# Two-block hybrid forward pass on one core: clamps, squares and probability scaling move to ScalarE, branch counts become logarithms in the mask, and the SSD head buffers rotate through four places

## The chip, the cores and the metric

The kernel runs on one core of a Trainium2 chip. The metric is the device time of one execution in microseconds (us), lower is better. One core has TensorE (PE in the profile, with PEld for its weight loads), VectorE (DVE), ScalarE (ACT), GpSimd (POOL) and the queue of SyncE (SP) that issues the weight DMAs. All engines run their own instruction streams and meet only at semaphores.

## What is computed

An input of 256 tokens by 1024 features goes through two blocks. The parts of the reference that the change touches, in short:

```python
# first block, Mamba-2 SSD: 32 heads in 4 groups, chunks of 128 tokens
cs = cumsum(dA)                                     # per head, along the tokens
lmat = exp(where(i >= j, cs_i - cs_j, -inf))        # decays between tokens i and j
y = einsum(cb, lmat, xdt) + ...                     # 256 x 256 per head, lower triangle
# first block, RG-LRU: width 1280 = 10 blocks of 128
a_t = exp(log_a)
b_t = sqrt(-expm1(2 * log_a)) * (i_gate * u)        # needs a_t squared
h_t = a_t * h_{t-1} + b_t
# second block, two layers, each with retention, a top-k attention (DSA, 4 heads)
# and a dilated attention (8 heads, three patterns (128,1), (512,4), (2048,16))
for window, dilation in DIL_PATTERNS:
    p = exp(s - m); den = sum(p); o = p @ v / den; lse = m + log(den)
alpha = softmax(lses); o = sum(alpha * outs)
# which is one softmax in which key j counts as often as patterns reach it:
# p_j = count_j * exp(s_j - m) / sum_j count_j * exp(s_j - m)
```

Both blocks also have large projections (in, out, FFN). They make up nearly all of the arithmetic.

## The kernel before

**Weight tiles.** Every projection is cut into 191 tiles of at most 128 x 2048 fp32 values (`TILES`), in one order for the whole program. A tile arrives by DMA in one of three `raw` slots. ScalarE copies it to `w_hi` (a rounded fp32r value), then VectorE and GpSimd each compute a part of the rest, `w_lo = raw - w_hi`; `POOL_SHARE` says in eighths how much of a tile GpSimd takes. TensorE then makes each product three times (hi*hi, hi*lo, lo*hi): 48 matmuls of 128x256 for a full tile. `w_hi` and `w_lo` have three slots, and `LEAD` is 2: the split of tile i+2 waits for tile i-1 to be used up (`tile_used`).

**Order.** ScalarE, VectorE and GpSimd each go through `walk`: for tile i first `lead(i)` (the split of tile i+2), then `rest` (second half of the evacuation of tile i-1), then the stages that `stage_order` puts at "mid" of tile i, then `evac` (first half of the evacuation of tile i), then the "after" stages. TensorE does the stages of "mid" between the halves of its tile. Each engine works strictly in its program's order, so a wait holds everything behind it.

**The LRU stages** (tiles lx 1 to bc 3). For each of 10 blocks ScalarE computes two tanh, `lru_a` (exp) and another tanh; GpSimd squares `lru_a` into a half of `tmp[4]`; VectorE makes `lru_b` and a gated `lru_u` of them.

**The SSD stages** (tiles gate 0 to z 4). For each group g of 8 heads there are `ssd_load` (a DMA on ScalarE's queue that broadcasts the group's cumulative sums to all partitions in `cs_all`), `ssd_open` and four pairs of heads, one pair per tile: `ssd_decay(g, p)` builds the two heads' decays in two buffers of `tmp`, and one tile later TensorE's `ssd_val(g, p)` (8 small matmuls from `tmp` and `xdt`) uses them and VectorE's `ssd_val` adds the result into `xbc`. In `ssd_decay` VectorE computes min(cs_j - cs_i, 0) (two `ts` per head), ScalarE takes exp in place, and VectorE multiplies by the masked scores `cb_mask`. The buffer index is `2 + (2 * q + h) % 4` with q = 4g + p and h = 2p or 2p + 1, which comes to `tmp[2]` for every even head and `tmp[3]` for every odd one.

**The attention stages** (from tile dil_v 0 of each layer to out_2 1). There are three sets of four heads: "dil0", "dsa" and "dil1". `att(l, a, step)` runs over steps 0 to 5, each at another tile:
- steps 0 and 2: TensorE computes the scores of two heads, VectorE scales them, adds the mask (`c["union"]` or `keep`) and takes the negative row maximum, ScalarE takes exp.
- steps 1 and 3: VectorE normalises. For the dilated sets it first multiplies by the table `count` (0 to 3) with a row sum, then takes a reciprocal and multiplies the probabilities by it; for dsa the row sum comes with ScalarE's exp.
- steps 2 and 4: TensorE transposes the probabilities, ScalarE copies them to `probs_t`; steps 3 and 5: product with the values and evacuation.

At "mid" of tile dil_k 1 of a layer stand retention steps and `att(l, "dil0", 1)`; at "mid" of dil_q 1, `att(l, "dil0", 2)` and `att(l, "dsa", 0)`. VectorE's evacuation of tile dil_k 1 (`lk_t<-bank,rstd` in the profile) comes between the two. Semaphores are shared between kinds (`GOES_ON`), which only renames a wait.

In the profile all ScalarE activations have line L856, VectorE's tensor-tensor operations L1182, tensor-scalar L1186 and L1187, scalar-tensor-tensor L1190, GpSimd's L1705, matmuls L491 and transposes L499.

## Time and profile before

| | |
|---|---|
| median of 3 runs | 1372.14 us (1369.8 to 1372.83) |
| the profiled execution | 1372.57 us, of which the span of the trace is 1371.3 us |
| TensorE busy | 1256.6 us (92%) |
| VectorE busy | 922.8 us (67%) |
| ScalarE busy | 614.1 us (45%) |
| GpSimd busy | 475.3 us (35%) |
| mean granted TensorE clock | 0.957 of full |

How to read it: the span is 1.3 us shorter than the execution's own time, and what follows is worked out on the span. TensorE's busy share is high, but it is an average. The first block's small stages (from 40 to 320 us) and the attention stages (720 to 810 us and 1080 to 1172 us) have gaps in it; in the FFN stretches there are nearly none.

### The profile page before, as it was taken

How to read it: one execution, taken by the hardware profiler on the slowest of the kernel's cores; microseconds unless marked ns; L12 is line 12 of the kernel's file. 1: busy time of each engine (PE TensorE's matmuls, PEld its weight loads, DVE VectorE, ACT ScalarE, POOL GpSimd, SP SyncE). 2: the span in 40 equal slices, each digit the busy share in tenths (PEclk: the TensorE clock that was granted, in tenths of full speed). 3: DMA queues.
4: the chain of work that ended last, by engine and by line, in shares of the span. 5: the costliest groups of instructions: out<-in, count | busy, mean ns of one | idle time of the engine just before them, and what ended most of it. 6: DMA issues, size and time to landing. Idle time of an engine off the chain costs nothing.

```text
span 1371.3 us, 23257 instructions
## 1 busy us (share of the span) xinstructions
PE 1256.6 (92%) x9852; PEld 1213.1 (88%) x9852; DVE 922.8 (67%) x1246; ACT 614.1 (45%) x703; POOL 475.3 (35%) x170
## 2 busy tenths in 40 slices
PE   4998898898998999999987899999999878999996
PEld 3988788888998999999886789999999767999996
DVE  5789987886646655557688856555456796755554
ACT  5766443445634533335433454333344245533332
POOL 1644233446773211111544233222224442422221
PEclk9999899999999999999998999999989989999998
DMA  8434444443466555555334136555543323455540
GB/s 249 156 97 152 153 155 154 154 149 112 170 210 209 180 182 181 181 182 151 124 112 134 62 103 206 184 184 185 163 154 123 124 86 98 145 195 181 183 160 31
DMA packets 153974, 209.57 MB, mean 153 GB/s; under 512 B 7536, under 2 KB 134672, under 8 KB 153232
## 3 DMA queue, kind: packets, MB, share of 16 engines
q1 hardware_dynamic: 150080, 201.54, 45.3%
q10 hardware_dynamic: 3792, 6.55, 1.4%
q8 instruction: 78, 1.28, 0.4%
q14 instruction: 24, 0.20, 0.0%
HBM read 207.00 MB, written 1.08 MB: 152 GB/s over the span
## 4 chain that ended last, share of the span: by engine, by line
PE 64%; DVE 20%; ACT 8%; issue 5%; POOL 1%; DMA 0%; ACTq 0%; SPq 0%; DVEq 0%; POOLq 0%
PE bank L491 63%; ACT w_hi L856 3%; DVE w_lo L1182 3%; DVE xbc L1190 2%; DVE probs_dil L1190 2%; ACT tmp L856 2%; DVE tmp L1187 1%; PE bank L499 1%; DVE lru_u L1190 1%; DVE tmp L1190 1%; DVE tmp L1182 1%; POOL w_lo L1705 1%; ACT act_hi L856 1%; DVE residual L1182 1%; DVE work L1186 1%
## 5 line engine op out<-in xcount | busy, mean ns | idle before, releaser
L491 PE MATMUL bank<-act_hi,w_hi 128*128 128x256 f32 x2920 | 849.9, 291 | 34.3 <-DVE w_lo L1182 14.6
L491 PE MATMUL bank<-act_lo,w_hi 128*128 128x256 f32 x2920 | 836.7, 287 | 0.0
L491 PE MATMUL bank<-act_hi,w_lo 128*128 128x256 f32 x2920 | 835.6, 286 | 0.0
L491 PEld LDWEIGHTS bank<-act_hi,w_hi 128*128 128x128 f32 x2920 | 571.8, 196 | 47.2 <-issue 36.6
L491 PEld LDWEIGHTS bank<-act_lo,w_hi 128*128 128x128 f32 x2920 | 571.9, 196 | 1.1 <-issue 0.5
L491 PEld LDWEIGHTS bank<-act_hi,w_lo 128*128 128x128 f32 x2920 | 571.1, 196 | 0.0
L1182 DVE TENSOR_TENSOR w_lo<-raw,w_hi 128x2048 fp32r<-128x2048 f32 (+4 forms) x179 | 375.6, 2100 | 264.8 <-ACT w_hi L856 264.7
L856 ACT ACTIVATE w_hi<-raw 128x2048 fp32r<-128x2048 f32 (+1 forms) x191 | 360.5, 1890 | 373.2 <-PE bank L491 371.8
L1705 POOL TENSOR_TENSOR w_lo<-raw,w_hi 128x1280 fp32r<-128x1280 f32 (+6 forms) x94 | 318.7, 3394 | 433.9 <-ACT w_hi L856 433.9
L1705 POOL TENSOR_TENSOR act_lo<-tmp,act_hi 128x512 fp32r<-128x512 f32 x52 | 133.3, 2570 | 407.0 <-ACT act_hi L856 407.0
L1182 DVE TENSOR_TENSOR tmp<-bank,rstd 128x512 f32<-128x512 f32 x43 | 29.7, 691 | 52.6 <-PE bank L491 52.5
L856 ACT ACTIVATE tmp<-tmp 128x384 f32<-128x384 f32 (+1 forms) x48 | 25.6, 555 | 70.5 <-DVE tmp L1187 69.7
L856 ACT ACTIVATE act_hi<-tmp 128x512 fp32r<-128x512 f32 x55 | 34.1, 619 | 34.0 <-DVE tmp L1190 34.0
L491 PE MATMUL bank<-w_hi,act_hi 128*128 128x256 f32 (+1 forms) x128 | 37.8, 295 | 3.1 <-DVE lq_t L1182 3.1
L856 ACT ACT_TABLE_LOAD x28 | 35.9, 1283 | 4.0 <-issue 2.3
L491 PE MATMUL bank<-w_hi,act_lo 128*128 128x256 f32 (+1 forms) x128 | 36.4, 285 | 0.0
L491 PE MATMUL bank<-w_lo,act_hi 128*128 128x256 f32 (+1 forms) x128 | 36.4, 284 | 0.0
L1190 DVE SCALAR_TENSOR_TENSOR probs_dil<-probs_dil,consts 128x128 f32<-128x128 f32 (+1 forms) x32 | 36.2, 1168 | 0.0
L1190 DVE SCALAR_TENSOR_TENSOR xbc<-bank,params,xbc 128x255 f32<-128x255 f32 (+2 forms) x72 | 29.0, 473 | 3.7 <-ACT xbc L856 3.7
L1190 DVE SCALAR_TENSOR_TENSOR tmp<-tmp 128x512 f32<-128x512 f32 x43 | 30.4, 708 | 1.1
L491 PEld LDWEIGHTS bank<-w_hi,act_hi 128*128 128x128 f32 x128 | 26.0, 203 | 5.8 <-DVE lq_t L1182 3.9
L491 PE MATMUL bank<-tmp,xdt 128*64 128x256 f32 (+1 forms) x128 | 15.3, 360 | 17.0 <-DVE tmp L1182 12.1
(206 smaller groups left out, 903.3 us busy)
## 6 DMA issues: line engine op xcount, KB each, us to landing
raw<-in_w_in SPq DMA_DIRECT2D x64, 1024.0 KB, 5.3
raw<-in_w_up SPq DMA_DIRECT2D x32, 1024.0 KB, 5.4
raw<-in_w_down SPq DMA_DIRECT2D x32, 1024.0 KB, 4.9
raw<-in_w_ffn_in SPq DMA_DIRECT2D x22, 1024.0 KB, 5.1
raw<-in_w_out SPq DMA_DIRECT2D x12, 1024.0 KB, 4.9
raw<-in_w_ffn_out SPq DMA_DIRECT2D x11, 1024.0 KB, 4.9
raw<-in_w_out_ssm SPq DMA_DIRECT2D x8, 1024.0 KB, 4.8
raw<-in_w_out_lru SPq DMA_DIRECT2D x5, 1024.0 KB, 4.8
```

Source lines behind the costliest of these rows:

```text
L491: return mm_ops.matmul(out, lhs, rhs, start=start, stop=stop, skip_group_check=True)
L499: return mm_ops.transpose(out, a, c["ident"][0:k, 0:k])
L856: return ops.activation(out, a, func, bias=bias, scale=scale, accum_out=accum)
L1182: return ops.tensor_tensor(out, a, b, op)
L1186: return ops.tensor_scalar(out, a, s1, None, op0)
L1187: return ops.tensor_scalar(out, a, s1, s2, op0, op1)
L1190: return ops.scalar_tensor_tensor(out=out, in0=a, scalar=s, in1=b, op0=op0, op1=op1, accum_out=accum)
L1705: return nc.gpsimd.tensor_tensor(out, a, b, op)
```

## The change

It does five things.

1. **Decays on ScalarE.** In `ssd_decay` ScalarE computes Relu(cs_i - cs_j) itself (two activations per head, scale -1, the column of `cs_tok` as bias) and then exp with scale -1. VectorE keeps only the product with `cb_mask`. `neg_cs` becomes `cs_tok`.
2. **Four places.** The buffers of a pair are `tmp[2 + h % 4]`: pairs alternate between `tmp[2], tmp[3]` and `tmp[4], tmp[5]`. ScalarE waits for the value product of the pair before the last one only.
3. **Squares on ScalarE.** The square of `lru_a` is an activation right behind the last tanh; GpSimd has no `lru` stage left.
4. **Counts as logarithms.** The mask `union` holds log(count), so exp gives count * exp(s - m) at once, with its row sum from ScalarE's accumulator. The table `count` and VectorE's product with it go away.
5. **Scaling on ScalarE.** VectorE takes only the reciprocal of the sums (`_r`); ScalarE multiplies the probabilities by it (`_n`), for all three sets of heads.

```diff
@@ build, buffers of a pair (PE, ACT and DVE alike) @@
-                    e = tmp[2 + (2 * q + h) % 4]
+                    e = tmp[2 + h % 4]
@@ act_program: lru @@
                 fn(r, r, ACT.Tanh, scale=lam, bias=lam).then_inc(*tick("lru_tl"))
+                act.wait_ge(*at("lru_b", h - 1))
+                fn(tmp[4][:, (h % 2) * SEQ:(h % 2 + 1) * SEQ], lru_a[:, h, :], ACT.Square).then_inc(*tick("lru_sq"))
@@ act_program: ssd_decay @@
                 q = 4 * g + p
+                act.wait_ge(sem("cs_broadcast"), 16 * (g + 1))
+                act.wait_ge(*at("dt_tok", 1))
+                act.wait_ge(*at("ssd_val", q - 1))
                 for h in (2 * p, 2 * p + 1):
-                    e = tmp[2 + (2 * q + h) % 4]
+                    e, hh = tmp[2 + h % 4], g * HPG + h
+                    fn(e[:, 0:SEQ], cs_all[:, h, :], ACT.Relu, scale=-1.0, bias=cs_tok[:, 0, hh:hh + 1])
+                    fn(e[:, SEQ:KQ], cs_all[:, h, P:SEQ], ACT.Relu, scale=-1.0, bias=cs_tok[:, 1, hh:hh + 1]).then_inc(
+                        *tick("ssd_d"))
+                for h in (2 * p, 2 * p + 1):
+                    e = tmp[2 + h % 4]
                     act.wait_ge(*at("ssd_d", HPG * g + h + 1))
-                    fn(e[:, 0:KQ], e[:, 0:KQ], ACT.Exp).then_inc(*tick("ssd_e"))
+                    fn(e[:, 0:KQ], e[:, 0:KQ], ACT.Exp, scale=-1.0).then_inc(*tick("ssd_e"))
@@ act_program: att @@
                         for n, x, y in PAIRS:
-                            inst = fn(p[:, x:y], p[:, x:y], ACT.Exp, bias=st[:, n:n + 1],
-                                      accum=None if dilated else st[:, 2 + n:3 + n])
+                            inst = fn(p[:, x:y], p[:, x:y], ACT.Exp, bias=st[:, n:n + 1], accum=st[:, 2 + n:3 + n])
                         inst.then_inc(*tick(f"{a}_e"))
+                if step in (1, 3):
+                    for h in heads[step - 1:step + 1]:
+                        s = 4 * l + h - heads[0]
+                        p, st = probs[a][s % 4], stats[a][s % 4]
+                        act.wait_ge(*at(f"{a}_r", s + 1))
+                        for n, x, y in PAIRS:
+                            inst = fn(p[:, x:y], p[:, x:y], ACT.Copy, scale=st[:, 4 + n:5 + n])
+                        inst.then_inc(*tick(f"{a}_n"))
@@ vec_program: ssd_decay @@
                 for h in (2 * p, 2 * p + 1):
-                    e, hh = tmp[2 + (2 * q + h) % 4], g * HPG + h
-                    vec.wait_ge(sem("cs_broadcast"), 16 * (g + 1))
-                    vec.wait_ge(*at("ssd_val", q - 1))
-                    ts(e[:, 0:SEQ], cs_all[:, h, :], neg_cs[:, 0, hh:hh + 1], ALU.add, 0.0, ALU.min)
-                    ts(e[:, SEQ:KQ], cs_all[:, h, P:SEQ], neg_cs[:, 1, hh:hh + 1], ALU.add, 0.0, ALU.min).then_inc(
-                        *tick("ssd_d"))
-                for h in (2 * p, 2 * p + 1):
-                    e = tmp[2 + (2 * q + h) % 4]
+                    e = tmp[2 + h % 4]
@@ vec_program: att @@
                         vec.wait_ge(*at(f"{a}_e", s + 1))
-                        if dilated:
-                            for n, x, y in PAIRS:
-                                inst = stt(p[:, x:y], p[:, x:y], 1.0, c["count"][:, x:y], ALU.mult, ALU.mult,
-                                           accum=st[:, 2 + n:3 + n])
-                            inst.then_inc(*tick("dve_step"))
-                            vec.wait_ge(*now("dve_step"))
-                        ops.reciprocal(st[:, 4:6], st[:, 2:4]).then_inc(*tick("dve_step"))
-                        vec.wait_ge(*now("dve_step"))
-                        for n, x, y in PAIRS:
-                            inst = ts(p[:, x:y], p[:, x:y], st[:, 4 + n:5 + n], ALU.mult)
-                        inst.then_inc(*tick(f"{a}_n"))
+                        ops.reciprocal(st[:, 4:6], st[:, 2:4]).then_inc(*tick(f"{a}_r"))
@@ pool_program @@
-            def lru(h):
-                pool.wait_ge(*at("lru_a", h + 1))
-                pool.wait_ge(*at("lru_b", h - 1))
-                tt(tmp[4][:, (h % 2) * SEQ:(h % 2 + 1) * SEQ], lru_a[:, h, :], lru_a[:, h, :], ALU.mult).then_inc(*tick("lru_sq"))
@@ shape_constants @@
-        "union": pairs(np.where(cnt > 0, 0.0, MASKED)), "count": pairs(cnt),
+        "union": pairs(np.where(cnt > 0, np.log(np.maximum(cnt, 1)), MASKED)),
```

How the instructions stand now. The first place is ScalarE's stream in the SSD stages, at tile ly 0, as a piece of the difference; `cs_all` and `cs_tok` are the cumulative sums, `tmp_2` to `tmp_5` the decays of a pair, `w_hi` the split of the tile two ahead.

```order
 L856 ACTIVATE w_hi_2<-raw_2 128x2048 [waits raw_arrived_2]
 L856 ACTIVATE tmp_0<-tmp_0 128x512 [waits ly_arg]
-L856 ACTIVATE tmp_2<-tmp_2 128x384 [waits ssd_d]
-L856 ACTIVATE tmp_3<-tmp_3 128x384 [waits ssd_d]
+L856 ACTIVATE tmp_4<-cs_all,cs_tok 128x256 [waits ssd_val]
+L856 ACTIVATE tmp_4<-cs_all,cs_tok 128x128
+L856 ACTIVATE tmp_5<-cs_all,cs_tok 128x256
+L856 ACTIVATE tmp_5<-cs_all,cs_tok 128x128
```

The two exps waited for VectorE (`ssd_d`); now four activations stand in front of them, of which the first waits for TensorE (`ssd_val`), and the exps follow in the new buffers.

The second place is VectorE's stream at "mid" of tile dil_k 1 and "mid" of dil_q 1 in the attention of the first layer, before:

```order
L1182 TENSOR_TENSOR ro_t<-ro_t,bank_3 128x256 [waits ro,gn_mean]
L1190 SCALAR_TENSOR_TENSOR probs_dil0_0,small<-probs_dil0_0,consts_2 128x128 [waits ssd_e]
L1190 SCALAR_TENSOR_TENSOR probs_dil0_0,small<-probs_dil0_0,consts_2 128x256
L1639 RECIPROCAL small<-small 128x2 [waits dve_step]
L1186 TENSOR_SCALAR probs_dil0_0<-probs_dil0_0,small 128x128 [waits dve_step]
L1186 TENSOR_SCALAR probs_dil0_0<-probs_dil0_0,small 128x256
...
L1182 TENSOR_TENSOR lk_t<-bank_1,rstd 128x512 [waits tile_used]
L1603 RECIPROCAL rq_t<-rq_t 128x256 [waits ly_tanh]
L1190 SCALAR_TENSOR_TENSOR rq_t<-rq_t,params,rg_t 128x256 [waits rg,dve_step]
```

And the same place after the change (the line numbers are those of the changed file):

```order
L1199 TENSOR_TENSOR ro_t<-ro_t,bank_3 128x256 [waits ro,gn_mean]
L1643 RECIPROCAL small<-small 128x2 [waits ssd_e] x2
L1199 TENSOR_TENSOR lk_t<-bank_1,rstd 128x512 [waits tile_used]
L1613 RECIPROCAL rq_t<-rq_t 128x256 [waits ly_tanh]
L1207 SCALAR_TENSOR_TENSOR rq_t<-rq_t,params,rg_t 128x256 [waits rg,dve_step]
```

Ten instructions of two heads are two now, and the evacuation `lk_t` stands right behind them.

The third place is ScalarE's stream at "mid" of tile dil_v 1, in the second layer, as a piece of the difference.

```order
 L856 ACTIVATE act_hi<-bank_6 128x256 [waits dil0_o]
-L856 ACTIVATE probs_dil1_0<-probs_dil1_0,small 128x128 [waits z_arg]
-L856 ACTIVATE probs_dil1_0<-probs_dil1_0,small 128x256
-L856 ACTIVATE probs_dil1_1<-probs_dil1_1,small 128x128 [waits z_arg]
-L856 ACTIVATE probs_dil1_1<-probs_dil1_1,small 128x256
+L856 ACTIVATE probs_dsa_0<-probs_dsa_0,small 128x128 [waits lru_gu]
+L856 ACTIVATE probs_dsa_0<-probs_dsa_0,small 128x256
+L856 ACTIVATE probs_dsa_1<-probs_dsa_1,small 128x128 [waits lru_gu]
+L856 ACTIVATE probs_dsa_1<-probs_dsa_1,small 128x256
```

Four scalings of dsa stand ahead of the exps of dil1, which now also write their row sums.

## Rows read from the trace of the kernel before

**Rows 1.** The page of the profile, TensorE's busy time and the chain that ended last.

```profile
PE 1256.6 (92%) x9852; PEld 1213.1 (88%) x9852; DVE 922.8 (67%) x1246; ACT 614.1 (45%) x703; POOL 475.3 (35%) x170
...
PE 64%; DVE 20%; ACT 8%; issue 5%; POOL 1%; DMA 0%; ACTq 0%; SPq 0%; DVEq 0%; POOLq 0%
```

**Rows 2.** Waits of the whole program: total us, times, longest.

```profile
ACT tmp L856 <- DVE tmp L1187: 69.7, 16, 5.0
...
PE bank L491 <- DVE lk_t L1182: 14.3, 2, 7.2
...
PE bank L499 <- ACT probs_t L856: 6.9, 2, 3.5
```

**Rows 3.** Four stretches: length, busy time of each engine, granted clock (PEclk), DMA.

```profile
157.00:306.00 149.00, 132.46 (x1024) 124.49 (x1024) 125.38 (x182) 66.01 (x89) 57.42 (x18) 0.94 0.47 149
315.70:322.50 6.80, 3.12 (x10) 2.76 (x11) 4.96 (x6) 6.59 (x9) 4.59 (x3) 0.50 0.51 157
745.80:756.00 10.20, 6.27 (x26) 4.00 (x27) 8.92 (x23) 3.63 (x8) 1.59 (x2) 0.50 0.38 130
203.00:207.00 4.00, 4.00 (x36) 4.00 (x35) 3.72 (x2) 0.18 (x1) 2.40 (x1) 1.00 0.04 14
```

**Rows 4.** Timeline of ScalarE, VectorE and GpSimd, one SSD step (199 to 208.5 us).

```profile
199.66 0.99 ACT L856 ACTIVATE tmp<-tmp 128x384 f32<-128x384 f32 x2 [3.26 <-DVE tmp L1187]
...
201.27 1.91 ACT L856 ACTIVATE w_hi<-raw 128x2048 fp32r<-128x2048 f32 x1
...
203.25 2.40 POOL L1705 TENSOR_TENSOR w_lo<-raw,w_hi 128x1024 fp32r<-128x1024 f32 x1 [5.77 <-ACT w_hi L856]
...
203.28 3.46 DVE L1182 TENSOR_TENSOR w_lo<-raw,w_hi 128x1024 fp32r<-128x1024 f32 x1 [2.03 <-ACT w_hi L856]
...
206.66 0.47 DVE L1190 SCALAR_TENSOR_TENSOR xbc<-xbc,params,bank 128x256 f32<-128x256 f32 x1
...
207.05 1.00 DVE L1187 TENSOR_SCALAR tmp<-cs_all,neg_cs 128x256 f32<-128x256 f32 x4
...
207.62 0.98 ACT L856 ACTIVATE tmp<-tmp 128x384 f32<-128x384 f32 x2 [4.44 <-DVE tmp L1187]
```

**Rows 5.** TensorE's waits, 160 to 307 us and 315 to 325 us.

```profile
PE bank L491 <- DVE tmp L1182: 12.5, 12, 2.0
...
PE bank L491 <- DVE tmp L1182: 6.1, 1, 6.1
```

**Rows 6.** Timeline of VectorE, GpSimd and TensorE in the first layer's attention.

```profile
737.60 4.70 DVE L1190 SCALAR_TENSOR_TENSOR probs_dil<-probs_dil,consts 128x128 f32<-128x128 f32 x1
...
742.23 4.71 DVE L1190 SCALAR_TENSOR_TENSOR probs_dil<-probs_dil,consts 128x256 f32<-128x256 f32 x1
...
747.65 0.28 DVE L1190 SCALAR_TENSOR_TENSOR probs_dil<-probs_dil,consts 128x128 f32<-128x128 f32 x1
...
748.99 0.68 DVE L1182 TENSOR_TENSOR lk_t<-bank,rstd 128x512 f32<-128x512 f32 x1
...
737.52 9.14 POOL L1705 TENSOR_TENSOR w_lo<-raw,w_hi 128x2048 fp32r<-128x2048 f32 x2 [8.03 <-ACT w_hi L856]
...
749.73 1.22 PE L491 MATMUL bank<-rk_t,consts 128*128 128x256 f32 x2 [7.17 <-DVE lk_t L1182]
```

**Rows 7.** Timeline of ScalarE in the same attention, and at tile lx 4.

```profile
739.13 0.41 ACT L856 ACTIVATE rk_t<-ro_t 128x256 f32<-128x256 f32 x1
...
754.44 1.49 ACT L856 ACTIVATE probs_dil<-probs_dil,small 128x128 f32<-128x128 f32 x4
...
772.01 0.80 ACT L856 ACTIVATE probs_dil<-probs_dil,small 128x128 f32<-128x128 f32 x2 [5.02 <-DVE small L1626]
...
61.20 0.47 ACT L856 ACTIVATE tmp<-bank,params 128x256 f32<-128x256 f32 x1 [0.66 <-PE bank L491]
```

**Rows 8.** Groups by line: busy us, mean ns, idle before them.

```profile
L1190 DVE SCALAR_TENSOR_TENSOR probs_dil<-probs_dil,consts 128x128 f32<-128x128 f32 (+1 forms) x32 | 36.2, 1168 | 0.0
...
L1187 DVE TENSOR_SCALAR tmp<-cs_all,neg_cs 128x256 f32<-128x256 f32 x64 | 22.9, 418 | 0.0
...
L1705 POOL TENSOR_TENSOR tmp<-lru_ab 128x256 f32<-128x256 f32 x10 | 10.5, 1053 | 13.2 <-ACT lru_ab L856 13.2
...
L856 ACT ACTIVATION_READ_ACCUMULATOR probs_dsa<-probs_dsa,small 128x1 f32 x16 | 3.1, 196 | 0.0
```

More of the change, by code:

```diff
@@ L82 @@
 CONSTS_2 = [("rotate", P), ("cos", SEQ), ("sin", SEQ), ("cos_k", SEQ), ("sin_k", SEQ), ("decay", RET_H * SEQ),
-            ("causal", KQ), ("union", KQ), ("count", KQ)]
+            ("causal", KQ), ("union", KQ)]
 def tile_names():
@@ L277 @@
     "dil0_pt": ("xbc_tanh", 12), "dsa_e": ("gate", 8), "dsa_hi": ("mix_hi", 4),
-    "ckv_n": ("cs", 1), "dil0_p": ("ssd_d", 32), "dil0_max": ("ssd_m", 32), "dil0_n": ("ssd_y", 16),
-    "dil0_lo": ("lru_out", 5), "dsa_p": ("lru_scan", 10), "dsa_max": ("lru_b", 10), "dsa_n": ("lru_gu", 10),
-    "dsa_lo": ("gn_x", 8), "dil1_p": ("z", 8), "dil1_max": ("z_arg", 8), "dil1_n": ("ly_arg", 5),
+    "ckv_n": ("cs", 1), "dil0_p": ("ssd_xdt", 8), "dil0_max": ("ssd_m", 32), "dil0_n": ("n1_sq", 4), "dil0_r": ("ssd_y", 16),
+    "dil0_lo": ("lru_out", 5), "dsa_p": ("lru_scan", 10), "dsa_max": ("lru_b", 10), "dsa_n": ("x1_hi", 4), "dsa_r": ("lru_gu", 10),
+    "dsa_lo": ("gn_x", 8), "dil1_p": ("z", 8), "dil1_max": ("z_arg", 8), "dil1_n": ("sp_exp", 2), "dil1_r": ("ly_arg", 5),
     "dil1_lo": ("ly_gelu", 5), "sel_acc": ("xbc", 12),
@@ L366, in build @@
         dt_tok = sb("dt_tok", [P, TT, HEADS], stack=one)
-        neg_cs = sb("neg_cs", [P, TT, HEADS], stack=one)
+        cs_tok = sb("cs_tok", [P, TT, HEADS], stack=one)
         lru_w = xbc[:, 0:2 * LC * P // SEQ, :].rearrange("p k (a j) -> p (k a) j", j=P).rearrange(
@@ L1354, in dt_turn @@
                 ops.tensor_copy(dt_tok[:, :, :], view[:, 0])
-                ts(neg_cs[:, :, :], view[:, 1], -1.0, ALU.mult).then_inc(*tick("dt_tok"))
+                ops.tensor_copy(cs_tok[:, :, :], view[:, 1]).then_inc(*tick("dt_tok"))
             def lru(h):
@@ L1630, in att @@
                         s = 4 * l + h - heads[0]
[L1631 removed]
+                        st = stats[a][s % 4]
                         vec.wait_ge(*at(f"{a}_e", s + 1))
[L1633 to L1643 removed]
+                        ops.reciprocal(st[:, 4:6], st[:, 2:4]).then_inc(*tick(f"{a}_r"))
                 if step in (3, 5):
@@ L1758, in pool_program @@
             low_part(4, 2, pair(tmp[8][:, :])).then_inc(*tick("x1_lo_pool"))
-            walk(lead, lambda i, name, j: None, rest, {"lru": lru, "norm_split": norm_split, "lru_split": lru_split,
-                                                       "ret": ret, "final": final})
+            walk(lead, lambda i, name, j: None, rest, {"norm_split": norm_split, "lru_split": lru_split, "ret": ret,
+                                                       "final": final})
         pe_program()
```

1 line of the change is left out of this document (removed).

## The prediction, made before the changed kernel ran

> **What bounds the kernel now.** The page comes first: TensorE is busy for 92% of the span and has 64% of the chain that ended last, but VectorE has 20% of that chain and ScalarE 8% [rows 1]. So most of the time is matmul time, which the change does not touch (TensorE's program is the same), and what can be won are the places where TensorE stands still or runs at the lower clock. The waits say where these are. ScalarE waited 69.7 us in 16 pieces for the clamps of the SSD decays (one for each pair of heads), TensorE 14.3 us in two pieces for `lk_t` and 6.9 us in two for `probs_t`, once in each layer [rows 2].
>
> The SSD stretch from 157 to 306 us is 149.0 us long, and TensorE is busy for 132.5 of them, so it idles 16.5 us. The granted clock is 0.94 there, which is 1.2 instead of 2.4 GHz for 12% of the time, 17.9 us; TensorE is busy for 89% of that and loses half, 8.0 us [rows 3]. Together 24.5 us could be had at most. TensorE's waits for the masked decays are 12.5 us of it, and one more of 6.1 us stands behind the stretch [rows 5].
>
> Why it idles is read from one step [rows 4]. ScalarE's `w_hi` starts at 201.27 and takes 1.91. VectorE's and GpSimd's `w_lo` start together at 203.25, and VectorE's takes 3.46 where GpSimd's takes 2.40: VectorE waits for GpSimd and then does its own part. Then come the product's addition to `xbc` (0.47), the clamps, and at 207.62 the exps, before which ScalarE had waited 4.44. The next `w_hi` stands behind these exps. The exps are 7.96 us apart (199.66 to 207.62): it is a ring through ScalarE, GpSimd and VectorE, and not TensorE, that sets the pace. TensorE's own work for such a step is 48 large matmuls, at 36 in 4.00 us [rows 3] 5.3 to 5.8 us, and the 8 small ones, for which I put 1.0: 6.8 us. The ring is 1.2 us longer.
>
> In the attention the picture is one of blocking. GpSimd splits two tiles back to back for 9.14 us from 737.52. VectorE's products with `count`, which read two tensors of SBUF, take 4.70 and 4.71 us in that time, and 0.28 when GpSimd is idle. So `lk_t` comes only at 748.99 and TensorE, which needs its bank, stands still for 7.17 us [rows 6]. Behind it the clock is 0.50 for 10.2 us [rows 3].
>
> **The change part by part.**
>
> *What goes from VectorE.* 64 clamps, 22.9 us, and 32 products with `count`, 36.2 us [rows 8]; with the 48 scalings, at 0.28 each as the nearest of their size [rows 6] 13.4, it is 72 us of 923. *What comes to ScalarE.* No activation with this input existed; the nearest are four exps of 128 and 256 columns in SBUF with a per-partition operand, 1.49 us [rows 7]. 16 pairs of decays are 23.8 us, 48 scalings 17.9 us, 10 squares at 0.41 are 4.1 us, and 32 reads of the accumulator at 0.196 [rows 7, 8] are 6.3 us: 52 us on 614. Bounds: if the clamp costs nothing beyond its cover, 0; if each costs what a lone 128x256 one does, 0.41, it is 64 x 0.41 = 26 us.
>
> *SSD: the ring breaks.* ScalarE's clamps wait only for TensorE's product two pairs back, because there are four buffers. So exps no longer wait for VectorE, and the next `w_hi` starts when TensorE has used up a tile. ScalarE's work for a step is then 1.91 + 1.49 + 0.98 and an evacuation, for which I put 0.9, 5.3 us, and 6.0 with another tanh, below TensorE's 6.8. VectorE has, after `w_hi`, 3.46 + 0.47 + 1.0 for the masked product, 4.9 us. Both fit, and TensorE becomes the bound. I take 14.0 of the 16.5 us of idle time and 6.0 of the 8.0 us of clock: 20.0. The two buffers alone would change little, the waits are for VectorE and not for a buffer. The wait of 6.1 us behind it [rows 5] hangs on ScalarE reaching the square root of the first group's norm, which stands behind the last exps; these exps waited for clamps that GpSimd blocked. I put it down to 1.4, so 4.7 more. **SSD: -24.7 us.** From both sides: 12 if only the clamps' own time (16 x 1.0, less what was hidden) goes from the ring, 30 if every gap closes and the clock's 1.6 us at 315.7 [rows 3] go too.
>
> *Attention, each layer.* Two reciprocals of two columns stand where 11.4 us of products and scalings stood (737.60 to 748.99 [rows 6]), so `lk_t` follows TensorE at once and 7.2 us go. The half clock behind it costs half of 6.27 busy us, 3.1. ScalarE's four scalings (1.49) delay the `w_hi` behind them, which has room: GpSimd works until 746.7 on the two splits. The wait for `probs_t` (3.5) is that of ScalarE for the maxima of dil1, 5.02 us [rows 7], that is for a VectorE that was late; it is less late, but ScalarE has eight more scalings (3.0 us) in front of these exps, which I see eat part. I take 2.5 of 3.5. Later ScalarE's scalings of dsa and dil1 stand four to a half tile of TensorE, and I count 1.0 us back for them. 7.2 + 3.1 + 2.5 - 1.0 = 11.8, **two layers: -23.6 us.** Bounds: 7.2 a layer, if the clock and the second wait stay and 1.0 more is lost (12), and 14 a layer (28).
>
> What could be late next: VectorE's `rq_t` product with `rg_t`, also of two SBUF tensors, now reaches the place of GpSimd's splits earlier. If it starts behind the start of a split, it waits up to 4.7 us as the `count` products did. That is the risk to the second wait.
>
> *LRU.* GpSimd loses 10 squares (10.5 us) and ScalarE gains 4.1 us. In tiles lx 3 and lx 4 ScalarE has two blocks in a tile and only 0.66 us of waiting in front [rows 7], so 2 x 0.41 comes through once or twice, and its `w_hi` and the softplus behind it get later. VectorE is blocked less by GpSimd. **+1.5 us**, from -1 to +3.
>
> *Everything else* (FFN, projections) has the same instructions; the mask with logarithms costs the same addition as the one of zeros.
>
> The sum is -24.7 - 23.6 + 1.5 = -46.8 us. I take off 2.8 for waits that take the place of those that go and that I can't name: -44. Against the profiled execution's 1372.6 that is 1328.6; the median of the three runs is 0.4 lower, so **1328 us**.
>
> Two rules of the Trainium skill bear on it. "GPSIMD Engine Reference", section "8. Key points", says that GpSimd shares its SBUF interfaces with VectorE and contends with instructions that have two SBUF inputs or run in the two-port mode; the 4.70 against 0.28 us above is such a case, and the clamps are of the second kind. "ScalarE: Activation LUTs", section "Rules for kernel authors", speaks against the change: relu and multiplication belong on VectorE. By rows, four clamps took 1.00 there [rows 4] and I give ScalarE 1.49; going by this rule the sum would be 16 x 0.49 = +7.8 us for the clamps, which would hold if both engines were equally full.
>
> **The rivals.**
>
> *A. Only one of the two parts pays (20%).* The attention's gain is eaten by ScalarE's order: `w_hi` and `probs_t` stand behind scalings that wait for a reciprocal, which waits for a blocked VectorE instruction. For it: 4.7 us for each such block. Against: in the trace the blocked products stand behind the sums, which are there early. Then 1372.6 - 24.7 + 1.5 = 1349, and about the same if instead the SSD keeps its pace.
>
> *B. The split sets the pace (9%).* GpSimd's and VectorE's `w_lo` stay serial at 3.46, and TensorE's waits turn to `w_lo`. Then the ring loses only the clamps, 12 us, and in the attention, where GpSimd splits whole tiles, VectorE's next two-tensor instruction takes the blocked one's place: 1372.6 - 12 + 1.5 = 1362. Against: `w_lo` is made two tiles ahead.
>
> *C. ScalarE becomes the bound (6%), slower.* All its 52 us of added work lie on the path, in the SSD tiles with a tanh and in the attention: 1328.6 + 52 = 1380. It decides for slower from 44 us exposed, and in the SSD from a step of ScalarE above 7.96 us; it is 5.3 to 6.0 by rows. (The rule on VectorE for relu in "ScalarE: Activation LUTs" of the Trainium skill points this way.)
>
> *D. No change (3%).* VectorE's relief all lies beside matmuls. The 7.17 us wait speaks against it.
>
> **How the numbers follow.** The forecast has 62%, with its own range of 1318 to 1342 from the bounds of its parts. For 8 in 10 the range reaches down to 1316 (every gap and clock piece gone, and LRU's -1) and up to 1352, over case A. A measurement of this kernel can tell about 0.2%, 2.7 us. Faster by more: 62 + 20 + 9, less 1 for B ending there, 90%; within it 4%; slower 6%.
>
> **What would show it.** In the new trace: ScalarE's waits for VectorE's clamps gone and its exps 6.8 us apart; TensorE's 7.17 us waits for `lk_t` under 1 us and full clock behind them; VectorE near 850 us, ScalarE near 665; waits for `probs_t` 1 us each. The prediction would be wrong if TensorE waits for `w_hi` or `w_lo` in the SSD, if a blocked VectorE instruction stands before each reciprocal, or if four clamps or scalings cost above 2.5 us.

## The result, and the profile after

The changed kernel takes 1314.25 us (median of 4 runs, 1314.09 to 1314.49), the kernel before 1371.66 on the same chip (4 runs, 1369.8 to 1372.83). The ratio is 0.958, 95% interval 0.957 to 0.960: 57.4 us faster, where 44 were forecast, and 1.8 us below the range's lower end of 1316. One execution of `ssd_only` below took 5210 us where its other four took 1339 to 1342, a slow state of the chip, and is left out of its numbers.

The page of the changed kernel, the lines that answer to [rows 1], with the granted clock in 40 slices between them:

```profile
PE 1235.0 (94%) x9852; PEld 1196.2 (91%) x9852; DVE 847.4 (65%) x1070; ACT 657.1 (50%) x857; POOL 464.3 (35%) x160
...
PEclk9999899999999999999889999999989899999998
...
PE 78%; DVE 13%; ACT 6%; issue 2%; DMA 1%; POOL 0%; ACTq 0%; SPq 0%; DVEq 0%; POOLq 0%
```

TensorE runs the same 9852 matmuls, but is busy for 21.6 us less than before: that is time at 1.2 GHz that became time at 2.4 (the clock's records have 118 us at the lower level before and 63 after). Its idle time is the span less the busy time: 1371.3 - 1256.6 = 114.7 before, 1313.2 - 1235.0 = 78.2 after, 36.5 less. So the 58.1 us of the span are 36.5 of idle time and 21.6 of clock. VectorE is busy for 75 us less, part of it time in which it was held up, and ScalarE for 43 more.

TensorE's waits in the changed kernel (total us, times, longest):

```profile
PE bank L491 <- DVE w_lo L1199: 17.0, 7, 4.3
PE bank L491 <- DVE tmp L1199: 13.7, 4, 9.0
PE bank L491 <- ACT act_hi L856: 10.4, 2, 7.6
PE bank L491 <- DVE rq_t L1199: 7.6, 2, 3.8
PE bank L491 <- DVE act_lo L1207: 5.3, 8, 1.1
PE bank L499 <- DVE act_lo L1199: 4.0, 4, 1.8
```

Against [rows 2] the waits for `lk_t` (14.3) and for `probs_t` (6.9) are gone, those for `tmp` fell from 31.3 to 13.7 in the whole program, 12.5 + 6.1 of the 31.3 in the SSD [rows 5], and ScalarE's 69.7 us for the clamps stand in no row any more. The waits for `act_lo` at transposes (L499) rose from 1.1 to 4.0, 1.8 of them at one place in each layer that had 0.6 before, and those for `w_lo` from 14.6 to 17.0, none of them in the SSD.

The SSD in windows (columns as in [rows 3]); the first stretch is nearly seven tiles long:

```profile
190.80:237.40 46.60, 46.60 (x389) 43.95 (x388) 38.13 (x35) 33.39 (x61) 21.97 (x8) 1.00 0.57 178
160.00:291.00 131.00, 130.07 (x1076) 123.10 (x1077) 113.56 (x126) 90.86 (x153) 61.88 (x21) 1.00 0.57 180
```

TensorE's value products, one group in each step, stand 6.75 us apart:

```profile
201.96 0.88 PE L491 MATMUL bank<-tmp,xdt 128*64 128x256 f32 x8
...
208.71 0.88 PE L491 MATMUL bank<-tmp,xdt 128*64 128x256 f32 x8
```

So it is for eleven of the twelve steps within the groups of heads (the last one has 7.61); before, they were 7.4 to 9.5 us apart. ScalarE's exps are 4.7 to 8.2 us apart, since it now runs ahead. In the first window TensorE is busy all the time at the full clock, ScalarE for 72% (4.8 us of a step) and VectorE for 82% (5.5). And one step's timeline, to be laid beside [rows 4]:

```profile
213.42 1.91 ACT L856 ACTIVATE w_hi<-raw 128x2048 fp32r<-128x2048 f32 x1
...
215.41 3.46 POOL L1705 TENSOR_TENSOR w_lo<-raw,w_hi 128x1536 fp32r<-128x1536 f32 x1 [3.24 <-ACT w_hi L856]
...
215.43 3.98 DVE L1199 TENSOR_TENSOR w_lo<-raw,w_hi 128x512 fp32r<-128x512 f32 x1 [1.39 <-ACT w_hi L856]
...
219.33 0.47 DVE L1207 SCALAR_TENSOR_TENSOR xbc<-xbc,params,bank 128x256 f32<-128x256 f32 x1
...
220.97 0.84 ACT L856 ACTIVATE lru_ab<-bank,params 128x256 f32<-128x256 f32 x2 [5.64 <-PE bank L491]
...
223.50 1.49 ACT L856 ACTIVATE tmp<-cs_all,cs_tok 128x256 f32<-128x256 f32 x4
...
224.88 0.93 ACT L856 ACTIVATE tmp<-tmp 128x384 f32<-128x384 f32 x2
```

The split still stands in a row: VectorE's quarter of `w_lo` takes 3.98 us beside GpSimd's 3.46. It no longer matters, because ScalarE does not come back to VectorE for its clamps: its idle time now ends with TensorE (5.64), and the exps follow the clamps at once.

TensorE's 9852 matmuls stand in the same order in both traces, so each stretch can be cut at the start of the same matmul in both. What became shorter (a minus is longer), in us:

| stretch of the kernel before | shorter by | of it idle time | of it busy time (clock) | forecast: idle, clock |
|---|---|---|---|---|
| 0 to 152.0 (with the LRU) | -2.7 | -3.7 | 1.0 | -1.5 |
| 152.0 to 326.6 (SSD) | 30.8 | 21.3 | 9.5 | 18.7, 6.0 |
| 326.6 to 704.3 | -1.5 | 0.0 | -1.5 | none |
| 704.3 to 803.9 (attention) | 14.6 | 9.25 | 5.3 | 8.7, 3.1 |
| 803.9 to 1062.0 | 1.6 | 0.0 | 1.5 | none |
| 1062.0 to 1166.1 (attention) | 15.1 | 9.25 | 5.8 | 8.7, 3.1 |

The two windows of the second row are these, the kernel before first:

```profile
152.00:326.61 174.61, 151.15 (x1148) 142.02 (x1149) 143.89 (x201) 81.97 (x105) 68.71 (x23) 0.92 0.47 151
```

```profile
154.70:298.48 143.78, 141.64 (x1148) 134.17 (x1149) 125.66 (x137) 102.88 (x169) 68.53 (x23) 0.98 0.56 180
```

### The profile page after: what moved, and what is told of

Same layout as the page of the kernel before. It is cut to its first block, busy times and chain, and to the rows that moved or that the text cites. A ratio compares the mean times of both kernels' runs of the same rounds, so it can differ in the third digit from the quotient of the medians.

```text
span 1313.2 us, 23221 instructions
## 1 busy us (share of the span) xinstructions
PE 1235.0 (94%) x9852; PEld 1196.2 (91%) x9852; DVE 847.4 (65%) x1070; ACT 657.1 (50%) x857; POOL 464.3 (35%) x160
## 4 chain that ended last, share of the span: by engine, by line
PE 78%; DVE 13%; ACT 6%; issue 2%; DMA 1%; POOL 0%; ACTq 0%; SPq 0%; DVEq 0%; POOLq 0%
PE bank L491 77%; DVE w_lo L1199 2%; ACT w_hi L856 2%; DVE xbc L1207 1%; ACT tmp L856 1%; ACT act_hi L856 1%; ACT L856 1%; PE bank L499 1%; DVE residual L1199 1%; DVE work L1203 1%; DVE act_lo L1207 1%; DVE tmp L1199 1%; DVE score L1199 1%; DVE rk_t L1199 1%; DVE tmp L1207 1%
## 5 line engine op out<-in xcount | busy, mean ns | idle before, releaser
L491 PE MATMUL bank<-act_hi,w_hi 128*128 128x256 f32 x2920 | 847.7, 290 | 36.5 <-DVE w_lo L1199 17.0
L1199 DVE TENSOR_TENSOR tmp<-tmp 128x512 f32<-128x512 f32 x28 | 20.4, 730 | 13.7 <-ACT tmp L856 12.1
L856 ACT ACTIVATE probs_dil<-probs_dil,small 128x128 f32<-128x128 f32 x64 | 26.2, 447 | 5.9 <-DVE small L1636 5.3
L856 ACT ACTIVATE tmp<-residual 128x512 f32<-128x512 f32 x32 | 18.5, 621 | 20.5 <-DVE residual L1199 13.6
```

What stands on the lines that cost most here:

```text
L491: return mm_ops.matmul(out, lhs, rhs, start=start, stop=stop, skip_group_check=True)
L856: return ops.activation(out, a, func, bias=bias, scale=scale, accum_out=accum)
L1199: return ops.tensor_tensor(out, a, b, op)
```

## The experiments

Fifteen further kernels ran, one of them the changed kernel again, on four chips and in 4 to 12 executions each. Each is compared with the kernel before on the same chip (its median was 1371.9 to 1373.0). A gain in us is the ratio's distance from 1, times 1372.

### Each part alone

`att_only` is the kernel before with the logarithms of the counts and ScalarE's scalings; `ssd_only` has ScalarE's decays and the four places; `squares_only` the LRU's squares on ScalarE; `no_squares` is the changed kernel with the squares back on GpSimd:

```diff
+            def lru(h):
+                pool.wait_ge(*at("lru_a", h + 1))
+                pool.wait_ge(*at("lru_b", h - 1))
+                tt(tmp[4][:, (h % 2) * SEQ:(h % 2 + 1) * SEQ], lru_a[:, h, :], lru_a[:, h, :], ALU.mult).then_inc(*tick("lru_sq"))
```

> The kernel before with the attention's part of the change alone (counts in the mask as logarithms, ScalarE scales the probabilities). Theory (the parts add, each gap of TensorE closes together with the low clock behind it): the trace of the changed kernel moves by 14.6 and 15.0 us in the two attentions, so 1371.7 - 29.6 = 1342. The prediction's own term was 23.6: 1348. Rival A (the parts need each other: ScalarE's scalings stand behind blocked VectorE instructions): 1372 to 1360.

> The kernel before with the SSD's part alone (decays on ScalarE, four places). Theory: everything from 157 us to the end of the SSD closes, all 16.5 us of idle time and the clock's pieces, 28 to 30 us: 1371.7 - 29 = 1343, with 1347 by the prediction's term of 24.7. Rival (the split sets the pace, as VectorE's and GpSimd's halves of w_lo stay serial): 12 us, 1360. Rival (ScalarE's clamps cost more than put down and stretch the LRU tiles' end): gain below 20, above 1352.

> The kernel before with the ten LRU squares on ScalarE alone. Theory: +1.5 us, 1373, of which the first gap behind the first LRU matrix product is 1.2 (in the changed kernel's trace it is 2.77 against 1.58), and the rest of the shift by clock. Rival (GpSimd's squares block VectorE, so their move gains): 1371.7 - 3 = 1369. Rival (no change): 1371.7.

> The changed kernel with the ten LRU squares back on GpSimd. Theory: the squares cost 1.5 to 2.7 us on ScalarE, so 1314.3 - 2 = 1312.3, faster than the changed kernel. Rival (relief of GpSimd is part of what the SSD gained, as the excess over the prediction is there): 1317 or more. Rival (no effect): 1314.3.

| kernel | median us | ratio to before | 95% interval |
|---|---|---|---|
| att_only | 1340.9 | 0.9771 | 0.9755 to 0.9787 |
| ssd_only | 1340.8 | 0.9769 | 0.9754 to 0.9784 |
| squares_only | 1372.6 | 0.9996 | 0.9983 to 1.0009 |
| no_squares | 1312.4 | 0.9565 | 0.9552 to 0.9579 |

Either part pays by itself, 31.4 and 31.7 us, as the two theories had it from the changed kernel's trace, so rival A (only one pays) falls, and with it B (the split sets the pace, 12 us for the SSD) and D (no change). The sum of the two, 63.1, is 3.4 more than both together give (59.7), which is no more than the three intervals leave open.

The squares alone make no difference that the times can tell, and taking them out of the changed kernel gives 0.9565 against 0.9583, with intervals that overlap. The traces can tell. From the matmul that starts at 60.0 us in the kernel before to the one at 152.0, all seven traces with the squares on ScalarE take 1.0 to 1.3 us longer than the kernel before, and the nine others without them differ from it by less than 0.2. TensorE's longest wait for `w_lo` there, in the kernel before, in `squares_only` and in the changed kernel:

```profile
95.28 0.55 PE L491 MATMUL bank<-act_hi,w_hi 128*128 128x256 f32 x1 [3.37 <-DVE w_lo L1182]
```

```profile
96.59 0.36 PE L491 MATMUL bank<-act_hi,w_hi 128*128 128x256 f32 x1 [3.97 <-DVE w_lo L1184]
```

```profile
98.02 0.55 PE L491 MATMUL bank<-act_hi,w_hi 128*128 128x256 f32 x1 [3.98 <-DVE w_lo L1199]
```

That is 0.6 us more behind a `w_hi` that stands behind one more activation of 0.4, and another 0.6 stands at the tile before, at 85 us. So the squares cost 1.2 us, by the way that the prediction named. The kernel without them, `no_squares`, is the better one.

Windows over the same matmuls show what went. First the kernel before, 1002 matmuls of the SSD with the wait behind it and the first attention with 602, then the same 1002 in `ssd_only`, and 603 in `att_only`:

```profile
177.65:326.61 148.96, 128.94 (x1002) 121.56 (x1001) 121.49 (x165) 69.77 (x89) 60.44 (x20) 0.94 0.45 146
...
704.30:803.90 99.60, 81.84 (x602) 71.99 (x601) 78.50 (x186) 42.08 (x73) 37.42 (x10) 0.90 0.33 106
```

```profile
173.11:295.82 122.71, 121.64 (x1002) 115.45 (x1001) 106.02 (x110) 86.13 (x140) 58.98 (x20) 1.00 0.55 176
```

```profile
704.20:789.20 85.00, 76.48 (x603) 68.38 (x601) 49.66 (x130) 51.65 (x113) 37.81 (x10) 0.96 0.38 124
```

In the SSD idle time (length less busy) falls from 20.0 to 1.1, by 18.9, and busy time by 7.3. In the attention idle time falls from 17.8 to 8.5, by 9.2, and busy time by 5.4. The forecast had 18.7 of idle time in the SSD (14.0 + 4.7) and 8.7 in a layer's attention (7.2 + 2.5 - 1.0): close, but the forecast's SSD began at 157 us and this window at 177.65; from 152 us on, the idle time of `ssd_only` falls by 20.7 and its busy time by 10.0 (21.3 and 9.5 in the changed kernel, as in the table above). The forecast had 6.0 and 3.1 of clock: too little.

### The attention's two halves

`counts_only` puts the logarithms into the mask, drops the products with `count` and leaves the scalings on VectorE. `scale_only` moves the scalings and keeps the products; the two edits together are `att_only`:

```diff
 # counts_only, VectorE
-                        if dilated:
-                            for n, x, y in PAIRS:
-                                inst = stt(p[:, x:y], p[:, x:y], 1.0, c["count"][:, x:y], ALU.mult, ALU.mult,
-                                           accum=st[:, 2 + n:3 + n])
```

> The kernel before with the counts moved into the mask as logarithms alone; VectorE still scales the probabilities. Theory (an instruction on two tensors of SBUF or in the two-port mode waits for GpSimd's split to end, and the scalings are such instructions): the scalings take the blocked place and most of the wait for lk_t stays, so a gain of 5 to 15 us of the 31.4 of both: 1373 - 10 = 1363. Rival (the products with count are the whole cost, the scalings run unblocked): 1373 - 29 = 1344.

> The kernel before with the scalings on ScalarE alone; VectorE still multiplies by count and sums. Theory: the two blocked products of 4.7 us stay, only what stood behind them goes, so TensorE's wait for lk_t falls from 7.2 us by at most 2 in each layer: 1373 - 4 = 1369. Rival (either half of the edit frees VectorE enough): 1373 - 20 = 1353.

1363.7 us (0.994, 0.993 to 0.995) and 1366.1 us (0.996, 0.994 to 0.997): 8.4 and 5.9 us, where both edits together gave 31.4. VectorE's timeline of `counts_only`, at the place of [rows 6]:

```profile
735.58 0.16 DVE L1633 RECIPROCAL small<-small 128x2 f32<-128x2 f32 x1
735.77 9.15 DVE L1186 TENSOR_SCALAR probs_dil<-probs_dil,small 128x128 f32<-128x128 f32 x2
...
745.50 0.68 DVE L1182 TENSOR_TENSOR lk_t<-bank,rstd 128x512 f32<-128x512 f32 x1
```

Two scalings take 9.15 us where the two products had taken 4.70 and 4.71; the next two, at 745.03 with GpSimd idle, take 0.55. So those 9.4 us did not belong to the product but to whatever instruction of that kind came first beside GpSimd's two splits, and TensorE's wait for `lk_t` falls from 7.17 to 5.51 us only. In `scale_only` another thing happens:

```profile
737.45 4.67 DVE L1198 SCALAR_TENSOR_TENSOR probs_dil<-probs_dil,consts 128x128 f32<-128x128 f32 x1
...
742.05 0.41 DVE L1198 SCALAR_TENSOR_TENSOR probs_dil<-probs_dil,consts 128x256 f32<-128x256 f32 x1
...
746.22 4.74 DVE L1198 SCALAR_TENSOR_TENSOR rk_t<-rq_t,ro_t 128x256 f32<-128x256 f32 x1
```

One product is held up and the second is not, because ScalarE's scalings stand in front of the `w_hi` of the next tile and wait for this blocked VectorE: GpSimd's second split starts at 746.13, not right behind the first. The wait for `lk_t` falls to 1.65 us, not by "at most 2" as expected, but the late split now holds up `rk_t`, and TensorE waits 4.16 us for `lq_t` where it had waited 0.78. This is the mechanism of rival A, and it takes back more than half of what `lk_t` gained. With both edits nothing is left beside the first split that could be held up: in `att_only` TensorE waits 0.78 us for `lq_t` and for `lk_t` not at all. That is why the gain of the two small edits together is more than twice their sum. The Trainium skill, "SBUF — State Buffer", section "SBUF: two separate sides", has it as an exclusive lock between GpSimd and a VectorE instruction that runs in a two-port mode or reads two SBUF inputs, which whichever of the two starts first holds for its whole instruction; the two times 4.6 us, each one split long, agree.

`dil_unsplit` takes the other way out. It is the kernel before, with GpSimd's splits taken away and the products left:

```diff
-              "dsa_q": 5, "ret_k": 5, "ret_q": 5, "ret_v": 5, "ret_g": 5, "dil_k": 7, "dil_q": 7, "dil_v": 8,
-              "out_2": 8}
+              "dsa_q": 5, "ret_k": 5, "ret_q": 5, "ret_v": 5, "ret_g": 5, "dil_k": 0, "dil_q": 0, "dil_v": 0,
+              "out_2": 0}
```

> The kernel before with the w_lo of dil_k, dil_q, dil_v and out_2 made by VectorE alone, so that GpSimd splits nothing beside the products with count; VectorE has 10 x 2.1 - 1.7 = 19 us more in each layer. Theory (blocking): the products take 0.28 and 0.42 us, TensorE's wait for lk_t falls from 7.2 by 8.7 less the two new splits of 2.1, to 2.7 us, with half the clock piece: 1372 - 12 = 1360. Rival (VectorE's own load is what makes lk_t late): slower, 1380 or more.

1367.6 us (0.996, 0.995 to 0.997), 5.3 faster. VectorE makes the splits as well and is still busy for 908.9 us only, against 922.8, since nothing holds it up there. Its timeline:

```profile
740.77 0.29 DVE L1190 SCALAR_TENSOR_TENSOR probs_dil<-probs_dil,consts 128x128 f32<-128x128 f32 x1
...
740.98 0.42 DVE L1190 SCALAR_TENSOR_TENSOR probs_dil<-probs_dil,consts 128x256 f32<-128x256 f32 x1
...
743.45 0.68 DVE L1182 TENSOR_TENSOR lk_t<-bank,rstd 128x512 f32<-128x512 f32 x1
```

The same products take 0.29 and 0.42 us: blocking it is, not VectorE's load. TensorE's wait for `lk_t` falls from 7.2 to 3.1 us (2.7 expected). That the gain is 5 and not 12 us is the price of the splits that VectorE now makes, which I had counted only up to `lk_t`: matched matmul by matmul, the first layer is 6.6 us shorter up to 760 us and 3.1 longer from there to 804, with a wait for `lq_t` of 2.1 where it had been 0.8.

### Places, and how much room ScalarE has

`places_only` is the kernel before with four places; `two_places` is the changed kernel with two, so that ScalarE's clamps wait for the pair just before:

```diff
-                act.wait_ge(*at("ssd_val", q - 1))
+                act.wait_ge(*at("ssd_val", q))
...
-                    e, hh = tmp[2 + h % 4], g * HPG + h
+                    e, hh = tmp[2 + (2 * q + h) % 4], g * HPG + h
```

> The changed kernel with the decays in two places instead of four; ScalarE's clamps then wait for TensorE's product of the pair just before. Theory (what mattered is the engine, not the places): TensorE's product, four clamps (1.8 us), two exps (0.9) and VectorE's masked products (1.0) make 4.7 us, below TensorE's step of 6.7: 1314 to 1319. Rival (the places break the ring): the steps go back to 8 us, 16 x 1.3 = 21 us more: 1335.

> The kernel before with the decays in four places, the clamps still on VectorE. Theory (VectorE is late and not the buffer): no change, 1373. Rival (the buffer's wait is part of the ring): 5 to 10 us faster.

1372.4 us (1.0003, 0.999 to 1.001) and 1315.6 us (0.9585, 0.957 to 0.960): the rotation gives nothing that the times can tell, with the clamps on either engine. "The two buffers alone would change little" holds.

`clamps_twice` and `clamps_thrice` let ScalarE compute every clamp once and twice more, into a spare tile:

```diff
+                    spare_h = spare[:, (h % 2) * KQ:(h % 2 + 1) * KQ]
+                    fn(spare_h[:, 0:SEQ], cs_all[:, h, :], ACT.Relu, scale=-1.0, bias=cs_tok[:, 0, hh:hh + 1])
+                    fn(spare_h[:, SEQ:KQ], cs_all[:, h, P:SEQ], ACT.Relu, scale=-1.0, bias=cs_tok[:, 1, hh:hh + 1])
```

> The changed kernel once more, on the same chip as the next three. Both theories: 1314 to 1315.

> The changed kernel with every clamp of the SSD computed once more by ScalarE into a spare tile (28.4 us of added ScalarE work, 1.77 in a step). Theory (TensorE sets the step of 6.66 us, ScalarE's 4.77 has 1.9 of room): 0 to 3 us slower, 1314 to 1317. Rival C of the prediction in its general form (ScalarE's work lies on the path): all 28 us appear, 1342.

> The same with every clamp computed three times (56.8 us added, a step of ScalarE is 4.77 + 3.54 = 8.3 us). Theory: past TensorE's 6.66, so ScalarE sets the pace: 16 x 1.65 = 26 us of idle time, and the low clock comes back in pieces of 3.4 us with the gaps of 1.3 to 2 us, 5 to 9 us more: 1345 to 1350. Rival (the work hides in other waits as it does when doubled): below 1325.

1313.1 us for the changed kernel (0.9575, 0.956 to 0.959), 1318.2 (0.961, 0.960 to 0.963) and 1336.0 (0.975, 0.973 to 0.976): 5 and 23 us more. Both expectations were off in size, in opposite directions. The added work was overstated: I had multiplied the mean duration of a clamp (0.44 us) by their number, but ScalarE's instructions overlap. And `clamps_twice`, with less work added than thought, cost 5 us and not 0 to 3. The windows of `clamps_twice` and `clamps_thrice`:

```profile
190.80:237.40 46.60, 45.94 (x382) 43.76 (x382) 37.54 (x36) 39.50 (x82) 21.75 (x7) 1.00 0.56 177
```

```profile
196.00:290.00 94.00, 86.58 (x715) 81.93 (x714) 71.14 (x73) 85.43 (x185) 42.83 (x13) 1.00 0.50 159
```

By the pages ScalarE is busy for 678.3 and 700.1 us against 657.1 in the changed kernel, so 64 more clamps add 21.2 us and 128 add 43.0: four more clamps add 1.3 us to a step, not 1.77. Doubled, TensorE's value products stay 6.7 to 7.0 us apart but for the first and the last step, and most of the 5 us come at the region's ends (2.2 between 157 and 190 us, and 3.2 behind 290, where TensorE waits 2.8 us where it had waited 1.1 behind the last step, with 3.4 us at the low clock). Tripled, they are 7.2 to 7.8 us apart in the window, as ScalarE's 4.8 + 2 x 1.3 = 7.4 would have it, and ScalarE is busy for 91% of the window. So rival C (ScalarE becomes the bound) has a place, but it lies two further sets of clamps away.

### ScalarE's scalings of dsa

In the changed kernel TensorE waits 1.8 us in each layer between two transposes, for an `act_lo` whose `act_hi` stands on ScalarE behind four scalings of dsa. `dsa_vector` gives dsa's scalings back to VectorE, `dsa_half` only those of the second pair of heads; both have the squares on GpSimd.

```diff
-                if step in (1, 3):
+                if step in (1, 3) and (dilated or step == 1):
...
+                        if not dilated and step == 3:
+                            vec.wait_ge(*now("dve_step"))
+                            for n, x, y in PAIRS:
+                                inst = ts(p[:, x:y], p[:, x:y], st[:, 4 + n:5 + n], ALU.mult)
+                            inst.then_inc(*tick("dsa_v"))
```

> The changed kernel with the squares back on GpSimd and the probabilities of dsa scaled by VectorE as before (those of dil0 and dil1 stay on ScalarE). In the changed kernel TensorE waits 1.8 us in each layer for act_lo behind ScalarE's four scalings of dsa (1.49), while VectorE is idle and GpSimd splits nothing. Theory: 1.5 us in each layer go: 1312.4 - 3 = 1309.4. Rival (VectorE's scalings are blocked by the split before, as the count products were): 1317 or more.

> The changed kernel with the squares on GpSimd and only the second pair of dsa's heads scaled by VectorE, where GpSimd splits nothing. Theory: the block of 2.6 us of dsa_vector stays away, and the wait behind the transposes falls from 2.0 to 0.8 us in each layer: 1312.4 - 2.5 = 1310. Rival (the wait moves on to the next one): 1312 to 1314.

`dsa_vector`: 1313.7 us (0.9577, 0.956 to 0.959), no gain. VectorE's timeline of its first pair, and TensorE's:

```profile
726.44 2.63 DVE L1202 TENSOR_SCALAR probs_dsa<-probs_dsa,small 128x128 f32<-128x128 f32 x2
```

```profile
735.92 0.93 PE L499 MATMUL bank<-consts,probs_dsa 128*128 128x128 f32 x6 [2.12 <-ACT probs_t L856]
```

The first pair's scalings fall beside a split and take 2.63 us for 0.55, everything behind them is late, and TensorE waits 2.12 us for `probs_t`: the rival's mechanism, at one of the two places. `dsa_half` avoids it: 1310.1 us (0.9544, 0.953 to 0.956). That is 0.3 to 0.4% faster than the changed kernel (0.9583 and 0.9575 on its two chips), clear of both intervals, and the fastest of all; but two edits are in it, and against `no_squares`, which has one of them, the gain is not clear of noise. Its trace has a wait of 1.10 in place of 1.77 us between the transposes, 0.7 a layer, where 1.2 was expected; the rest of its 0.0021 against `no_squares` (2.9 us) stands in its trace as shorter pieces of low clock, most of which begin ahead of the edited steps, and the two intervals overlap.

### What a gap costs

`stalls` is the changed kernel with seven gaps made in stretches that have none. Behind a tile GpSimd fills n tiles, and TensorE waits for it:

```diff
+            def stall(name, j, n):
+                pool.wait_ge(*now("stall"))
+                pool.wait_ge(*used(name, j))
+                for t in [t for a in probs for t in probs[a]][:n]:
+                    inst = nc.gpsimd.memset(t[:, :], 0.0)
+                inst.then_inc(*tick("stall"))
```

> The changed kernel with seven gaps made in TensorE's work in stretches that have none: TensorE waits behind seven tiles for GpSimd to fill 1, 2, 3, 4, 6, 8 and 12 tiles of 128x384. Theory (each gap from some length on brings low clock behind it): gaps of under 1 us bring none, gaps of 2 us and more bring each a piece of 3.4 or 6.8 us at the low clock, so 1.7 or 3.4 us on top of the gap, whatever its length. Rival (the low clock comes only where gaps follow each other): single gaps cost their own length alone, and no piece of low clock is seen behind them.

1331.4 us (0.970, 0.969 to 0.971). From the trace, each gap from matmul to matmul less the 0.12 us of a usual one, the piece at the low clock behind it, and by how much the matmuls behind both are later:

| gap us | 0.69 | 1.11 | 1.47 | 1.83 | 2.55 | 3.27 | 4.71 |
|---|---|---|---|---|---|---|---|
| low clock us | none | none | none | none | 3.4 | 3.4 | 6.8 |
| later us | 0.79 | 1.21 | 1.57 | 1.93 | 4.09 | 4.86 | 7.35 |

The fourth gap's stretch and the pieces behind the last three, in windows:

```profile
567.00:577.00 10.00, 8.33 (x69) 8.13 (x69) 2.98 (x2) 3.79 (x3) 1.56 (x5) 1.00 0.62 211
822.10:825.50 3.40, 3.27 (x15) 3.27 (x16) 2.07 (x1) 0.00 (x0) 0.08 (x1) 0.50 0.38 113
873.30:876.70 3.40, 3.40 (x17) 3.40 (x17) 1.04 (x1) 0.00 (x0) 0.00 (x0) 0.50 0.33 76
924.50:931.30 6.80, 5.80 (x27) 5.81 (x28) 0.78 (x1) 0.00 (x0) 0.94 (x3) 0.50 0.47 154
```

These gaps cost their own length up to 1.83 us, and 1.5 to 2.6 us more from 2.55 on. The first theory holds for the long ones; the rival (a single gap costs only its length) holds for the short ones. It is no rule by length alone. The same wait of 2.80 us stands ahead of the same matmul in the kernel before and in the changed one:

```profile
415.93 0.36 PE L491 MATMUL bank<-act_hi,w_hi 128*128 128x256 f32 x1 [2.80 <-ACT act_hi L856]
415.90:422.70 6.80, 6.77 (x56) 6.80 (x57) 5.21 (x8) 3.74 (x4) 1.23 (x1) 1.00 0.27 92
```

```profile
387.84 0.36 PE L491 MATMUL bank<-act_hi,w_hi 128*128 128x256 f32 x1 [2.80 <-ACT act_hi L856]
388.10:391.50 3.40, 3.40 (x18) 3.40 (x18) 3.27 (x6) 1.26 (x3) 0.00 (x0) 0.50 0.47 158
```

The one is followed by the full clock, the other by 3.4 us at half of it. What decides between them, these runs don't show.

## Why the forecast was right in kind and short in size

**The ring, and that TensorE becomes the bound: right.** The steps are 6.75 us (forecast 6.8), ScalarE's wait for clamps is gone, TensorE waits for no `w_lo` in the SSD, and `ssd_only` shows it alone.

**The blocked products: right.** `lk_t`'s waits are gone; `counts_only` and `dil_unsplit` show from both sides that GpSimd's splits made them. The risk that the prediction named, that `rq_t`'s product would be held up in their place, did not come, and by little: in the changed kernel `rk_t`, the instruction behind it, starts at 716.20 and 725.11 us, and GpSimd's splits at 716.37 and 725.18. `scale_only` shows what it costs when it comes. That part is luck.

**Idle time: nearly right in size.** 36.5 us less measured; the terms without clock give 18.7 + 2 x 8.7 - 1.5 = 34.6. The parts are less close: 21.3 in the SSD, 9.25 in each attention (of 3.5 us for `probs_t` nothing was left, where 1.0 had been kept), and -3.7 ahead of 152 us.

**The clock: the step that failed.** "I take ... 6.0 of the 8.0 us of clock" and "The half clock behind it costs half of 6.27 busy us, 3.1" make 6.0 + 2 x 3.1 = 12.2 us; the page shows 21.6. In the SSD 9.5 us went: all of the window's 8.0, and 1.6 behind the wait at 315.7, which I had only in the bound of 30. In the attentions 5.3 and 5.8 went, since a second piece of low clock, behind the wait for `probs_t` at 776.9, goes with that wait; I had read one piece (745.8). The other 1.0 us is pieces that moved outside the SSD and the attentions (1.0, -1.5 and 1.5 in the table). I had taken a share of the gaps and a smaller share of the clock, though the clock pieces stand behind those very gaps.

**The 2.8 us taken off "for waits that I can't name": wrong.** Outside the LRU the only waits that grew are the two of 1.8 us (by 1.2 each), and they are the "1.0 back" for ScalarE's scalings. With 9.4 us too little clock and 1.9 too little idle time that is the whole error: 44.0 + 9.4 + 1.9 + 2.8 = 58.1, the fall of the span. The same 2.8 is in the lower end of the range: the bounds of the parts add up to 30 + 28 + 1 = 59 us, which is 1313, and 1316 is that with 2.8 taken off.

**Prices.** VectorE 847 (forecast 850) and ScalarE 657 (665) came as said. Four clamps take 1.49 us as the four exps did. Part of the 8 us too many for ScalarE is that reads of the accumulator were counted at their full 0.196 us: the one at 729.89 takes 0.19, and the next exp starts at 729.99.

**LRU, +1.5: right, though the times can't tell it.** The squares cost 1.2 us between 60 and 152 us in all seven traces that have them, as waits for `w_lo`. The changed kernel's trace is 2.7 us later at 152; the other 1.5 are there from 40 us on and are clock: 16 matmuls at 39.9 us run in 3.4 us at half clock, where before 29 did at full clock. Kernels without the squares have this too (`no_squares` and `places_only` have a piece at 38.5 and are 1.0 later), and `squares_only` has none.

**The rule on relu.** The Trainium skill, "ScalarE: Activation LUTs", section "Rules for kernel authors", would leave relu and multiplication on VectorE. At its best a group of four clamps agrees: it took 1.00 us there [rows 4] and takes 1.49 here. Over the program the two are nearly equal, 22.9 us on VectorE [rows 8] against 16 x 1.49 = 23.8, because some of VectorE's were held up to 2.7 us while ScalarE's groups take 1.48 to 1.50 beside a split too. The kernel is 57 us faster, since VectorE stood in TensorE's way and ScalarE did not.

**What stays open.** Both parts together give 3.4 us less than their sum. In the traces `att_only` and `ssd_only` each gain the same 1.6 us at 1012, where a piece of low clock of 10.2 us becomes one of 6.8, which can be gained once only; `ssd_only` gains 1.4 us more in the two attentions, which it doesn't touch, and `no_squares` has a piece at 387 that neither part has. These pieces move with the phase of the run; that was read, not tested, and the difference is within the noise of the three times. How much of the SSD's ring was GpSimd's splits and how much the way through VectorE was not tested either: no run takes the splits of these tiles from GpSimd.

## What to carry to other kernels

Before costing an instruction by its mean, look for the ones that take ten times their usual time, and ask who runs beside them: removing one of them gives little when the next of its kind takes its place, so count the whole group up to the instruction that TensorE waits for. An operation that is slower on another engine can still pay, if that engine has room in each step and is outside the ring. And when gaps close, add the low clock behind every one of them, all along the program, from the busy time of the same matmuls and not from one window.
